# FFN up chunks as 256-column matmuls into one bank, and new SBUF places for matmul operands

## The reference

```
h = rms_norm(x, norm_g)
return (silu(h @ w_gate) * (h @ w_up)) @ w_down
```

## Time and profile before

| | |
|---|---|
| runs | 1046.49, 1046.62, 1046.79 us |
| profiled execution | 1044.18 us |
| its span, first to last instruction | 1042.4 us |
| TensorE clock granted in it | 1.0 of full |
| TensorE, VectorE, ScalarE busy | 99%, 83%, 64% of the span |

### The profile page before, as it was taken

The page is one execution under the profiler, slowest core; times in us unless marked ns, Lnnn a source line. Parts: engine busy times, 40 slices in busy tenths (PEclk is TensorE's granted clock), DMA queues, the critical chain, the costliest instruction groups (busy, mean ns, idle before and its releaser), DMA issues.

```text
span 1042.4 us, 19061 instructions
## 1 busy us (share of the span) xinstructions
PE 1034.8 (99%) x7330; PEld 958.1 (92%) x7330; DVE 862.8 (83%) x1083; ACT 671.1 (64%) x952; POOL 2.7 (0%) x8
## 2 busy tenths in 40 slices
PE   8999999999999999999999999999999999999998
PEld 7888999898888999999899999999899889999998
DVE  6878986687787856998988878798998899888786
ACT  6666565466555447676886767675546678667673
POOL 0000000000000000000000000000000000000000
PEclk9999999999999999999999999999999999999999
DMA  9942464354555564544545555454432565555541
GB/s 342 285 154 82 162 226 139 121 194 167 182 196 197 174 239 158 192 149 168 209 169 206 200 201 180 173 195 163 137 120 108 185 219 185 186 204 199 195 145 65
DMA packets 30529, 186.91 MB, mean 179 GB/s; under 512 B 3735, under 2 KB 6520, under 8 KB 8840
## 3 DMA queue, kind: packets, MB, share of 16 engines
q1 hardware_dynamic: 29896, 185.05, 50.8%
q10 hardware_dynamic: 576, 1.05, 0.3%
HBM read 183.96 MB, written 1.34 MB: 178 GB/s over the span
## 4 chain that ended last, share of the span: by engine, by line
PE 91%; DVE 5%; ACT 2%; issue 1%; DMA 1%; SPq 0%; DVEq 0%; ACTq 0%
PE g L552 60%; PE d L552 31%; DVE w_lo L1598 2%; DVE x L1595 1%; ACT w_hi L1084 1%; PE d L555 1%; DVE p_both L1602 1%; DMA raw<-weights 1%; DVE sq_sum L1595 1%; DVE gla_both L1602 0%; DVE ple_z L1592 0%; DVE ple_mul L1592 0%; PE g L555 0%; DVE conv_out L1595 0%; ACT gla_both L1084 0%
## 5 line engine op out<-in xcount | busy, mean ns | idle before, releaser
L1598 DVE TENSOR_TENSOR w_lo<-raw,w_hi 128x2048 fp32r<-128x2048 f32 (+1 forms) x175 | 389.3, 2227 | 57.8 <-ACT w_hi L1084 57.4
L1084 ACT ACTIVATE w_hi<-raw 128x2048 fp32r<-128x2048 f32 (+1 forms) x174 | 324.7, 1872 | 57.6 <-PE d L552 38.9
L552 PE MATMUL g<-f_both,w_hi 128*128 128x512 f32 x704 | 246.2, 393 | 0.0
L552 PE MATMUL g<-f_both,w_lo 128*128 128x256 f32 x704 | 197.2, 280 | 0.0
L552 PEld LDWEIGHTS g<-f_both,w_hi 128*128 128x128 f32 x704 | 131.8, 187 | 28.9
L552 PE MATMUL d<-hid_hi,w_hi 128*128 (+1 forms) x528 | 145.9, 276 | 0.0
L552 PE MATMUL d<-hid_lo,w_hi 128*128 (+1 forms) x528 | 145.9, 276 | 0.0
L552 PE MATMUL d<-hid_hi,w_lo 128*128 (+1 forms) x528 | 145.8, 276 | 0.0
L552 PEld LDWEIGHTS g<-f_both,w_lo 128*128 128x128 f32 x704 | 133.0, 189 | 0.1
L552 PEld LDWEIGHTS d<-hid_hi,w_hi 128*128 128x128 f32 x528 | 99.2, 188 | 0.9
L552 PEld LDWEIGHTS d<-hid_lo,w_hi 128*128 128x128 f32 x528 | 99.1, 188 | 0.0
(11 more groups left out here) (388 smaller groups left out, 2233.1 us busy)
## 6 DMA issues: line engine op xcount, KB each, us to landing
raw<-weights SPq DMA_DIRECT2D x168, 1024.0 KB, 4.8
bias_tab<-bias_dram SPq DMA_DIRECT2D x8, 192.0 KB, 7.7
x<-x_t ACTq DMA_DIRECT2D x4, 256.0 KB, 5.4
raw<-weights SPq DMA_DIRECT2D x4, 256.0 KB, 6.6
raw<-weights SPq DMA_DIRECT2D x2, 512.0 KB, 7.5
mem_t<-mem_t SPq DMA_DIRECT2D x1, 1024.0 KB, 9.5
out<-x SPq DMA_DIRECT2D x3, 256.0 KB, 2.1
hy_swap<-hy_qk SPq DMA_DIRECT2D x4, 128.0 KB, 6.0
```

What stands on the lines that cost most here:

```text
L552: return pe.matmul(out, lhsT, rhs, start=start, stop=stop, skip_group_check=True)
L1084: return act.activation(out, in_, func, **kw)
L1598: return dve.tensor_tensor(out, a, b, ALU.subtract)
```

## The change

1. Up chunks from the third on, in all three FFNs, take the form of `chunk`: three 256-column matmuls for each tile into one bank. The first two keep the pairs. In the first FFN norm_sum moves from behind the second chunk into its middle.
2. Their eviction is one VectorE product with rstd out of the bank; `low_halves`, `whole`, the low copies and the adds go for these chunks. ScalarE's taps and silu wait for `evicted`.
3. The six weight slots of w_hi and w_lo get 512 bytes more each, 3072 in all. The weights of listed chunks (`further`) start 32 bytes into their slot: the token chunks of w_in, w_cv and gla_in, the first three chunks of w_out, w_co and gla_out, the first two up chunks of each FFN. Other chunks start where the slot starts.
4. `*_both` tiles get new offsets: gla and mem 32; out, co, x0, f1, go, f2 192; in, hy, p stay at 32 and ho at 192. H and what lies in it shifts by 3072 bytes with the slots, a multiple of 512. A few small buffers move to make room.
5. In the embedding's first gate chunk norm_sum stands ahead of k = 6 instead of k = 4.

```diff
+FURTHER_COLS = 8
+W_SLOT = CHUNK + P
+def further():
+    chunks = {FIRST["w_in"] + j for j in (4, 5, 10, 11)}
+    chunks |= {FIRST["w_cv"] + j for j in range(4)}
+    chunks |= {FIRST["gla_in"] + j for j in range(4, 8)}
+    chunks |= {FIRST[name] + j for name in ("w_out", "w_co", "gla_out") for j in range(3)}
+    chunks |= {FIRST[name] + j for name in ("up0", "ffn1", "ffn2") for j in range(2)}
+    return chunks
+def start_col(c):
+    return FURTHER_COLS if isinstance(c, int) and c in FURTHER else 0
...
-        w_hi = sb("w_hi", [U, CHUNK], F32R)
-        w_lo = sb("w_lo", [U, CHUNK], F32R)
+        w_hi = sb("w_hi", [U, W_SLOT], F32R)
+        w_lo = sb("w_lo", [U, W_SLOT], F32R)
...
-        mem_both, MEM = parts_at("mem_both", B_AT)
-        out_both, OUT = parts_at("out_both", A_AT)
-        co_both, CO = parts_at("co_both", A_AT)
-        x0_both, X0 = parts_at("x0_both", B_AT)
+        mem_both, MEM = parts_at("mem_both", B_AT + 32)
+        out_both, OUT = parts_at("out_both", A_AT + 192)
+        co_both, CO = parts_at("co_both", A_AT + 192)
+        x0_both, X0 = parts_at("x0_both", B_AT + 192)
-        f1_both, F1 = parts_at("f1_both", A_AT)
+        f1_both, F1 = parts_at("f1_both", A_AT + 192)
-        gla_both, GLA = parts_at("gla_both", A_AT)
-        go_both, GO = parts_at("go_both", B_AT)
-        f2_both, F2 = parts_at("f2_both", A_AT)
+        gla_both, GLA = parts_at("gla_both", A_AT + 32)
+        go_both, GO = parts_at("go_both", B_AT + 192)
+        f2_both, F2 = parts_at("f2_both", A_AT + 192)
...
+        def weights_of(part, c, slot, cols=slice(0, CHUNK)):
+            at_col = start_col(c)
+            return part[:, slot, at_col + cols.start:at_col + cols.stop]
...
             def gated_chunk(j, jm):
+                if not isinstance(j, int) or j >= 2:
+                    chunk("up0", j, jm, X0)
+                    return
...
+                    elif k == KT // 2:
+                        norm_sum()
...
-                if early and j == 1:
-                    norm_sum()
...
                 def up(p, u):
...
+                            if early:
+                                to = UP[u][:, f, :]
+                                mm(to, hi, both[:, k, :, :].rearrange("p a t -> p (a t)"), k == 0, False)
+                                last = mm(to[:, 0:T], lo, both[:, k, 0, :], False, k == KT - 1)
+                            else:
+                                to = UP[u][:, 0, f * T:(f + 1) * T]
+                                mm(to, hi, both[:, k, 0, :], k == 0 and f == 0, False)
+                                mm(to, hi, both[:, k, 1, :], False, False)
+                                last = mm(to, lo, both[:, k, 0, :], False, k == KT - 1)
...
-                    chunk(f"gate{layer}", j, j % U, moving, fresh=j == 0, between=norm_sum, at_k=4 if j == 0 else None)
+                    chunk(f"gate{layer}", j, j % U, moving, fresh=j == 0, between=norm_sum, at_k=6 if j == 0 else None)
...
+                    mul(gated_z[:, :, jm, :], bank_of("up0", j, jm), over(rstd[:], 2)).then_inc(evicted, count.one(evicted))
...
+                def feed_from_bank(p, u):
+                    dve.wait_ge(chunk_done, up_place(p, u) + (FIRST[name] + 1))
+                    mul(conv_in[:, u, :, 2:2 + T], as_tiles(UP[u][:, 0, :]), over(rstd[:], 2)).then_inc(evicted, count.one(evicted))
...
                     hidden()
-                    whole(p, 0)
-                    feed(p, 0)
+                    feed_from_bank(p, 0)
                     split_at(p, 3)
                     middle_tap(p, 0)
                     hidden_low(p - 1)
-                    whole(p, 1)
-                    feed(p, 1)
+                    feed_from_bank(p, 1)
```

More of the change, by code:

```diff
@@ L211, in program @@
         par = sb("par", [N_PCOLS])
+        COS_AT = place["at"]
         cos_t = sb("cos_t", [T])
@@ L661, in chunk_k @@
                     m_hi, m_lo = (tile_at(m, k0 + h) for m in moving)
-                    mm(to, w_hi[:, slot, cols], m_hi, first and h == 0 and f % 2 == 0, False)
-                    mm(to, w_hi[:, slot, cols], m_lo, False, False)
-                    last = mm(to, w_lo[:, slot, cols], m_hi, False, final and h == 1)
+                    mm(to, weights_of(w_hi, c, slot, cols), m_hi, first and h == 0 and f % 2 == 0, False)
+                    mm(to, weights_of(w_hi, c, slot, cols), m_lo, False, False)
+                    last = mm(to, weights_of(w_lo, c, slot, cols), m_hi, False, final and h == 1)
                     if final and h == 1 and f in (1, 3, 5) and to_x:
@@ L1328, in gated_body @@
                     opening("up0")
-                act.wait_ge(chunk_done, j + (FIRST["up0"] + 1))
-                for bank, f in ((G, 0), (D, 1)):
-                    fn(gated_lo[:, jm, f, :], bank[(FIRST_OUT["up0"] + jm) % U][:, T:2 * T]).then_inc(lo_copied, 1)
+                if early and j < 2:
+                    act.wait_ge(chunk_done, j + (FIRST["up0"] + 1))
+                    for bank, f in ((G, 0), (D, 1)):
+                        fn(gated_lo[:, jm, f, :], bank[(FIRST_OUT["up0"] + jm) % U][:, T:2 * T]).then_inc(lo_copied, 1)
                 if early and j in (0, 2):
@@ L1335, in gated_body @@
                     ahead("up0", j, jm)
-                act.wait_ge(gate_done, count.next(gate_done))
+                if early and j < 2:
+                    act.wait_ge(gate_done, count.next(gate_done))
+                else:
+                    act.wait_ge(evicted, j + (FIRST_OUT["up0"] + 1))
                 fn(gate_act[:, jm, :], gate_z[:, jm, :], ACT.Silu).then_inc(act_done, 1)
@@ L1441, in outer_taps @@
                 def outer_taps(p, u):
-                    act.wait_ge(conv_fed, count.next(conv_fed))
+                    if isinstance(p, int) and p == 0:
+                        act.wait_ge(conv_fed, count.next(conv_fed))
+                    else:
+                        act.wait_ge(evicted, p * 2 + (FIRST_OUT[name] + u + 1))
                     for f in range(2):
@@ L1484, in body @@
                     gelu()
-                    low_halves(p, 0)
                     split_at(p, 3)
@@ L1987, in gated_hid @@
                 dve.wait_ge(act_done, count.next(act_done))
-                dve.wait_ge(up_scaled, count.next(up_scaled))
+                if isinstance(j, int) and j < 2:
+                    dve.wait_ge(up_scaled, count.next(up_scaled))
+                else:
+                    dve.wait_ge(evicted, j + (FIRST_OUT["up0"] + 1))
                 mul(hid[:, jm % U, :], gate_act[:, jm % U, :], up_z[:, jm % U, :]).then_inc(hid_done, count.one(hid_done))
@@ L2195, in body @@
                         hidden()
-                        whole(1, 1)
-                        for u in range(2):
-                            feed(1, u)
+                        feed_from_bank(1, 1)
                         split_at(2, 2)
@@ L2448, in _ @@
             first_half, second_half = slice(0, CHUNK // 2), slice(CHUNK // 2, CHUNK)
[L2449 removed]
+            sub(weights_of(w_lo, c, c % U, first_half), raw[:, c % U, first_half], weights_of(w_hi, c, c % U, first_half).bitcast(F32)).then_inc(dve_own, count.one(dve_own))
             gla_evict(11, split=False)
```

103 lines of the change are left out of this document (49 added, 54 removed).

## The result

The changed kernel takes 1054.13 us (median of 4 runs, 1054.08 to 1054.27), the kernel before 1046.7 in the same session (4 runs, 1046.49 to 1047.15). The ratio is 1.0082, 95% interval 1.007 to 1.0094: slower. The forecast was 1036.5 us and its range ended at 1052. The profiled execution of the kernel before lies 2.5 us under its median, that of the changed kernel doesn't, and what makes this difference isn't shown. The clock granted to TensorE was 1.00 in both.

What follows compares the result with a forecast made beforehand. TensorE's matmul pace was taken as the bound (busy 99% of 1042.4 us). Terms -7.0 - 2.4 + 0.1 (gla_in's first chunk) - 0.5 - 0.3 = -10.1 us from the 1046.62 median gave 1036.5 us, range 1033 to 1052.

Steps and rivals of the forecast that it cites:

- Moved chunks -7.0: 60 up chunks of the three FFNs go from 5.55 to 5.44 us, -6.6 us, and layer 2's slow start goes, -0.4.
- I take fast: Moved up chunks at distance 192 were taken to run at 113.3 ns a matmul, not the slow 117.8.
- the first rival: FFN up, down and two proj chunks stay at 117.8 ns a matmul: +10.2 us, 1056.8; two or three stages slow 0.27.
- It is set by how a stage is entered: Pace at distance 192: fast after pairs at 347 ns, slow after pairs at 353 ns or an fp32 matmul.
- distance 160: Kept pairs' moving operand start minus the stationary one's, modulo 256 bytes, after the change; 0 before.
- fast in all stages: All three FFNs at the fast pace: 1036.5 us, own range 1033 to 1040, chance 0.45.
- Places of other chunks -2.4: Outside the moved chunks, new offsets: 256-column chunks to distance 32 -1.5 us, last chunks to 192 -0.3, w_in's tokens -0.6.
- kept pairs -0.5: 240 pairs in 15 chunks go from distance 0 to 160; bounds -2.6 and +2.2 us, half of -1.0 taken.
- norm_sum -0.3: Gates' norm_sum at k=6 avoids a 0.27 us wait for squares in layer 2; layer 1 saves nothing.
- gla_in -1.0: Eight 256-column gla_in chunks go from distance 0 to 32, part of the -1.5 us; its first chunk gains nothing.
- Evictions 0: One VectorE product frees 1.3 us of two engines a chunk, hidden by 11 us before the bank's next use: 0.
- The form gives nothing: Rival: up chunks run near 116.7 ns a matmul, 5.60 us a chunk, +3.0, the rest -3.1: 1046.5 us, chance 0.12.

Runs made afterwards that it cites:

- the last microbenchmark: Only matmuls, most of the kernel left out: pairs with weights 32, 192 or 0 bytes further, then 256-column tiles; 353 ns a tile in 15 of 16, 340 in 16, 353 in 16.
- the microbenchmark: Only matmuls on copies of x, nine distances between parts and weights: steady 360 ns a tile at distance 0, 350 at 32, 340 or 353 at 192.

## Why the prediction was wrong, point by point

- **Moved chunks -7.0**, the step that failed: "I take fast". Measured is the first rival, the slow pace locked in, in all three stages: up 5.65 us a chunk as it had said, down 5.65, proj 5.65, so +12.2 us where -7.0 was forecast. It put the FFNs at +13.3 us; they cost +12.2, since the kept pairs and layer 2's start, slow before as well, gave some back. That rival's time was 1056.8 us, the measured is 1054.1; it had added its +10.2 to the median, and between the profiled executions +9.9 was measured.
- **The reason given for it.** "It is set by how a stage is entered" was right: 60 ns of matmul at the entry give 1034.4 us and weights moved at the entry 1034.9, near the forecast of 1036.5. What was wrong is the inference that pairs at a pace of 347 ns lead into the fast one. The pairs at 160 did run at 346.6, and led into the slow one in all three stages; so did pairs at 346.6 ns at the old places ahead of the first down chunk of layer 1, in the kernel with the new places alone. The entering operands' places matter (16 of 16 against 1 of 16 in the last microbenchmark, three stages of three in the kernel), but don't decide by themselves, as the two rows of w_out show. The prediction had noted that distance 160 was "shown by no row", and yet its chance of fast in all stages, 0.45, rested on an entry that the change itself replaced.
- **Which cover was removed.** In the kernel before, pairs at distance 0 came between any two down chunks, and behind them down ran at 113.5 ns in all but one case: layer 2's first down was slow, the next one fast again. In the changed kernel nothing brings the pace back. The first rival named this. It costs 32 down and two proj chunks x 0.21 us, which is 7 of the 12.2.
- **Places of other chunks -2.4, kept pairs -0.5, norm_sum -0.3.** Near in size as a sum: outside the FFNs 2.3 us were gained. That is in part luck, for gla_in gave less (next point) and layer 1's gates more. The prediction has layer 1 save nothing by norm_sum at k=6; its gates became 0.55 us shorter, and only 0.18 shorter with the new places and norm_sum left at k=4. w_ck runs at 4.44/38 = 116.8 ns in its first chunk, w_in's token matmuls at 227, and the gates' first 36 matmuls pass into k=6 with no gap (4.21 us where there had been one of 0.27). Part of the gain was lost again in waits. At w_out's first chunk border TensorE had got ahead by 0.84 us and VectorE's w_lo by 0.44, so a wait appeared that wasn't there:

```profile
124.66 0.28 PE L581 MATMUL d<-out_both,w_lo 128*128 128x256 f32 x1
125.38 0.50 PE L581 MATMUL d<-out_both,w_hi 128*128 128x512 f32 x1 [0.44 <-DVE w_lo L1638]
```

- **gla_in -1.0**, a term of the places, came to little, 0.1 us up to gla_out: from its start to the norm's matmul it took 11.40 us where it had been 11.13, and its last two chunks are at 10.61/90 = 117.9 ns, not 116.7. Distance 32 too has more than one level in the kernel, 350 and 353 ns a tile; in the microbenchmark it stayed at 350. Why isn't shown.
- **Evictions 0.** Right. VectorE's product reads the bank in 0.69 us, two chunks before the bank is used again, and no wait for an eviction ends a gap on TensorE:

```profile
593.67 0.69 DVE L1632 TENSOR_TENSOR conv_in<-g,rstd 128x512 f32<-128x512 f32 x1 [0.81 <-PE g L581]
```

- **The form gives nothing**, a rival at 1046.5, had the ups near 116.7 ns a matmul; they ran at 117.8, or at 113.3 with another entry. At distance 192 the form gains in the fast pace (340 against 347 ns a tile) and loses in the slow one (353), and at distance 0 it loses more (360).
- **A row misread.** gla_out's pairs before the change are given as 14.37/40.5 = 354.8 ns. The odd one of the 81 matmuls is a 512-column one, so it is more than half a pair; from start to start they were 353.3. Only the average of some 351 ns hangs on it, by under 1 ns.
- **The skill's rules.** By "TensorE: Matmul & The Clock Gate", Back-to-back issue gap, in the Trainium skill (N/2.4 + 2.5 ns), a moved tile takes 2.5 ns more than a pair. The section gives this formula for the isolated matmul, without the weight loads that stand ahead of each one here, which the prediction left unsaid. The runs say 340 (7 ns less) in the one pace and 353 (6 ns more) in the other. From the same page's separate read ports (What happens when you issue a matmul) the prediction had inferred that places would change nothing; 360, 350 and 340 ns a tile for one form at three distances, with the other engines nearly idle, say that they do.

What stays open is the mechanism inside TensorE: why one sequence of operands has two steady paces, and which entries lead to which. The runs give a list of cases, not a rule, and some entries went both ways with the same instructions.

## What to carry to other kernels

Where TensorE is the bound and its matmuls follow one another without a gap, read its pace as length by count in the chain of waits, and expect operands' places to matter by some per cent, and the same code to have more than one steady pace. A loop of one form kept whatever pace it entered with here, so a change that makes a loop uniform also removes what used to reset it: look at the entry, and test it with one short extra matmul or with the first weights at another place. How the old entry behaved was no guide to the one that the change put in its place. And compare stages that an edit doesn't touch: hy_out alone moved by 0.7 us between kernels.

## What the runs showed of the hardware that was not expected

- Tiles of three 256-column matmuls with operands 192 bytes apart, modulo 256, had two steady paces, 340.0 and 353.3 ns. Each lasted through as many as 1488 matmuls without a gap (20 chunks of up0 and 11 of down0), until something else came between.
- One matmul of 128 columns, 60 ns, moved 31 chunks behind it by 0.21 us each. At 6 of 23 places outside the FFNs the same matmul was followed by the slow pace.
- In the microbenchmark of borders the pace after a run of pairs went with the place of their weights in 47 of 48 entries, and no semaphore count or satisfied wait at the border changed it. In the kernel w_out's last chunk took either pace behind the same pairs.
- Token chunks, with the weights as the moving operand, took 226.7 ns a matmul with parts and weights at the same place modulo 256, 229 with the parts 192 bytes ahead of the weights, and 233 with them 32 to 160 ahead. There the same place is the best, where for the 256-column form it is among the worst (360 ns, as at 96).
